# Where the split weights live in SBUF: `wh` and `wl` moved from the middle to the top

## Chip, cores and metric

One Trainium2 chip, one core. Times are device microseconds of that core; the time of a kernel is the median of its runs. The engines are TensorE (PE, with its weight loads shown apart as PEld), VectorE (DVE), ScalarE (ACT), GpSimd (POOL) and SyncE (SP), which here only issues DMAs.

## What is computed

Four transformer layers on 512 tokens of width 1024, in fp32: two layers of `first_block`, then two of `second_block`. Each has a mixer and a gated feed-forward unit, with a normalised residual after either. Cut to the matrix products:

```
first layer:   h = rms_norm(x)*(1+sc)+sh;  parts = split(h @ w_in);  latent queries, sparse attention and mLSTM
               x += g * rms_norm(concat(att, hm) @ w_out)
               h = rms_norm(x)*(1+sc)+sh;  x += g * rms_norm((silu(h @ w_gate) * (h @ w_up)) @ w_down)
second layer:  h = rms_norm(x);  parts = split(h @ w_in);  compressed, selected and window attention, stick-breaking attention
               y = g_a*(o_nsa @ w_proj_nsa) + g_b*(o_sb @ w_proj_sb);  x += rms_norm(y @ w_out)
               h = rms_norm(x);  u = conv(h @ w_up);  x += rms_norm((gelu(gate) * up) @ w_down)
```

The hidden width of the feed-forward units is 2816.

## The kernel before

Activations lie feature-major: a tile such as `hh` is [128, 8, 512], 8 chunks of 128 features by 512 tokens, 2048 bytes a chunk in each partition. Every large product is computed in three passes. Weights and activations are each split in a rounded head and the rest: `wh` and `wl` for the weights, `hh` and `hl` (mixers, gate/up), `cqh` and `cql` (latent queries), `fnh`/`fnl` and `fsh`/`fsl` (features of the second mixer, in its projections) or `hidh` and `hidl` (down projection) for the activations. `three_pass` (L198 to L201) issues three fp32r matmuls into one PSUM bank: head by head (L199), the weights' head by the activations' rest (L200), the weights' rest by the activations' head (L201). Each matmul has its own weight load: 128 columns of `wh` or `wl` are loaded and stay, and the activations' 512 columns stream. In the profile's names the streaming tile stands first and the loaded one second, as in `bank<-hh,wh`.

The weights come as a stream of slots of 128 x 1024 (L136 to L195). SP fills the ring `raw` of four slots by DMA (L160). ACT writes the head of a half slot (512 columns) to `wh` (L171), POOL subtracts it from `raw` and writes `wl` (L182); both have room for two slots. TensorE waits for the half slot's `wl`, uses it in 12 matmuls, and releases it through `slot_done`; ACT then refills it for the slot after next. Semaphores for all of this are written out by hand, and the order of each engine is the order of the code.

Most products load weights and stream activations. In three places `wh` and `wl` stream instead, and activations are loaded: the token-major values of the first mixer (L831 to L833, 512 columns) and of the second (L1775 to L1777, 512 or 280 columns), and the compression product of the second mixer, where 128 columns of `wh` or `wl` stream against 32 columns of `peh` or `pel` (through `three_pass`, so also L199 to L201).

`Arena` (L91) hands out addresses in a partition one after the other, rounded up to 32 bytes. `fixed` begins at base0 and holds, in this order, `x`, `hh`, `hl`, `y`, `raw`, `wh`, `wl`, the constants `cst`, parameters, `cos`, `sin`, `sq`, `acc` and `tmp`. The top MIX = 90112 bytes, from mix0 on, are a region that the mixers and the gated units use in turn: `hidh` and `hidl` fill it in the gate/up and down stages; in the mixers it holds the attention's tiles (`qk`, `pr`, `vsw`, `peh`), and then `fnh` to `fsl`. Further arenas overlay `y`, `sq` and `tmp`. `product_out` (L289) is the product with 1024 output features that ends each mixer (streaming `hh`, `hl`) and each gated unit (streaming `hidh`, `hidl`); `gate_up` (L505) is the first half of a gated unit. L1692 transposes through an identity in `cst` that streams, with `pr` or `sq` loaded.

Of the kernel before, what the change touches and what calls it, by code (L numbers as in the profile page):

```python
# [7 lines left out]
F32R = mybir.dt.float32r  # L8
# [5 lines left out]
P = 128  # L14
# [8 lines left out]
SLOT = 1024  # L23
# [180 lines left out]
def build(nc, a, out):  # L204

    m = Mem()
    base0 = -(-nc.sbuf_base // 32) * 32
    total = nc.sbuf_usable_end // 32 * 32 - base0
    MIX = KF * T * 4 * 2
    fixed = Arena(nc, base0, total - MIX)  # L210
    mix0 = base0 + total - MIX
    m.x = fixed("x", [P, KD, T])
    m.hh = fixed("hh", [P, KD, T], F32R)
    m.hl = fixed("hl", [P, KD, T], F32R)
# [1 line left out]
    m.y = fixed("y", [P, KD, T])  # L216
    ring_at = fixed.at
    m.raw = fixed("raw", [P, RING, SLOT])
    m.wh = fixed("wh", [P, 2, SLOT], F32R)
    m.wl = fixed("wl", [P, 2, SLOT], F32R)  # L220
    RING_BYTES = fixed.at - ring_at
    m.cst = fixed("cst", [P, C_COLS])
    m.pc = fixed("pc", [P, B_COLS])
# [2163 lines left out]
def program(nc, a, out):  # L2387
    build(nc, a, out)
# [150 lines left out]
```

How the kernel before makes its waits and increments, by code:

```python
    def __call__(self, ins):  # L111
        self.n += 1
        ins.then_inc(self.sem, 1)
        self.eng.wait_ge(self.sem, self.n)
# [40 lines left out]
    def loads(self, sp, t0, t1):  # L155
        for t in range(t0, min(t1, self.total)):
            if t >= RING:
                sp.wait_ge(self.rest_ready, 2 * (t - RING) + 2)
            w_ = self.width(t)
            sp.dma_start(self.m.raw[:, t % RING, 0:w_], self.source(t)[:, 0:w_]).then_inc(self.w_in[t % RING], 16)
# [4 lines left out]
    def head(self, act, t, half):  # L165
        if half == 0:
            act.wait_ge(self.w_in[t % RING], 16 * (t // RING + 1))
        if t >= 2:
            act.wait_ge(self.slot_done[half], t - 1)
        w_ = self.part(t, half)
        act.activation(self.m.wh[:, t % 2, w_], self.m.raw[:, t % RING, w_], ACT.Copy)\
           .then_inc(self.head_ready, 1)
# [6 lines left out]
    def rest(self, pool, t, half):  # L179
        pool.wait_ge(self.head_ready, 2 * t + half + 1)
        w_ = self.part(t, half)
        pool.tensor_tensor(self.m.wl[:, t % 2, w_], self.m.raw[:, t % RING, w_],
                           self.m.wh[:, t % 2, w_].bitcast(F32), ALU.subtract)\
            .then_inc(self.rest_ready, 1)
# [6 lines left out]
    def ready(self, pe, t, half=1):  # L191
        pe.wait_ge(self.rest_ready, 2 * t + half + 1)
# [1 line left out]
    def done(self, eng, t):  # L194
        eng.wait_ge(self.slot_done[1], t + 1)
# [109 lines left out]
        def tensor(pe):  # L305
# [15 lines left out]
                if part == 0 and nb >= 2:  # L321
                    pe.wait_ge(square_ready, nb - 1)
                    pe.wait_ge(y_ready, nb - 1)
                c0 = 8 * part
```

## Time and profile before

| | |
|---|---|
| median of 3 runs | 3337.89 us (3336.79 to 3338.76) |
| the profiled execution | 3341.34 us, its span 3339.6 us |
| TensorE's mean granted clock in it | 0.959 |
| busy: PE, PEld | 3135.7 us (94%), 2473.8 us (74%) |
| busy: DVE, ACT, POOL | 1577.1 us (47%), 1274.4 us (38%), 1300.4 us (39%) |

Busy time of a matmul counts from its start to its end, and matmuls are pipelined, so that one that "takes" 389 ns is followed by the next long before it ends. How far apart they start is read from the start times. A row of the groups ends with the idle time of the engine before its instructions and what ended it.

### The profile page before, as it was taken

To read this page: it belongs to the slowest core of one execution; us is meant where nothing else is said; L and a number is where in the kernel's file an instruction comes from. 1 tells how busy PE (TensorE), PEld (TensorE's weight loads), DVE (VectorE), ACT (ScalarE), POOL (GpSimd) and SP (SyncE) were. 2 spreads that over 40 slices of the span, in tenths; PEclk is the share of its full clock that TensorE was granted. 3 is DMA by queue.
4 is the path that set the end of the run, shared out by engine and by line. 5 is a ranking of instruction groups with operands and counts; after the bars stand their busy time and mean duration, and the time that the engine had idled before them with its cause. 6 is when DMAs were issued, how large, how long until landed. Compare 5 with 4: busy or idle time off the path is not lost.

```text
span 3339.6 us, 39384 instructions
## 1 busy us (share of the span) xinstructions
PE 3135.7 (94%) x14764; PEld 2473.8 (74%) x14764; DVE 1577.1 (47%) x2533; ACT 1274.4 (38%) x2494; POOL 1300.4 (39%) x1118
## 2 busy tenths in 40 slices
PE   5998789998989989998999998999989999989998
PEld 3666668886767768886877786888868777768886
DVE  7687466612776354212344644554043345355521
ACT  3335332233345432233353533443234534344432
POOL 2331235543432234443541542544434334434443
PEclk8998789998999889999999998999989999989998
DMA  5422336732411122322321121333223211223222
GB/s 209 120 77 89 120 131 237 250 99 72 123 64 45 39 73 96 100 92 73 119 87 45 45 76 57 101 95 100 93 82 101 74 45 51 90 67 96 95 93 71
DMA packets 92829, 316.50 MB, mean 95 GB/s; under 512 B 12000, under 2 KB 12512, under 8 KB 92512
## 3 DMA queue, kind: packets, MB, share of 16 engines
q1 hardware_dynamic: 92640, 313.99, 29.0%
q8 instruction: 118, 1.93, 0.2%
q14 instruction: 71, 0.58, 0.1%
HBM read 301.36 MB, written 2.10 MB: 91 GB/s over the span
## 4 chain that ended last, share of the span: by engine, by line
PE 90%; DVE 5%; issue 2%; ACT 1%; DMA 1%; SPq 1%; POOL 0%; DVEq 0%; ACTq 0%; POOLq 0%
PE bank L199 24%; PE bank L201 23%; PE bank L200 23%; PE bank L1713 3%; PE bank L1671 2%; PE bank L1692 2%; PE bank L412 1%; PE bank L813 1%; PE bank L831 1%; PE bank L833 1%; PE bank L832 1%; PE bank L975 1%; DMA mod_raw<-in_wmod 1%; DVE x L479 1%; DVE tmp L477 1%
## 5 line engine op out<-in xcount | busy, mean ns | idle before, releaser
L182 POOL TENSOR_TENSOR wl<-raw,wh 128x512 fp32r<-128x512 f32 (+1 forms) x952 | 1240.8, 1307 | 1917.8 <-ACT wh L171 1915.4
L171 ACT ACTIVATE wh<-raw 128x512 fp32r<-128x512 f32 (+1 forms) x952 | 587.4, 623 | 1471.8 <-PE bank L201 1363.8
L199 PE MATMUL bank<-hh,wh 128*128 128x512 f32 x2496 | 1005.2, 403 | 71.1 <-DVE hl L456 46.0
L201 PE MATMUL bank<-hh,wl 128*128 128x512 f32 x2496 | 984.3, 394 | 0.0
L200 PE MATMUL bank<-hl,wh 128*128 128x512 f32 x2496 | 983.4, 394 | 0.0
L199 PEld LDWEIGHTS bank<-hh,wh 128*128 128x128 f32 x2496 | 476.5, 191 | 196.8 <-DVE hl L456 51.8
L201 PEld LDWEIGHTS bank<-hh,wl 128*128 128x128 f32 x2496 | 475.1, 190 | 102.4
L200 PEld LDWEIGHTS bank<-hl,wh 128*128 128x128 f32 x2496 | 476.7, 191 | 96.2 <-issue 0.5
L201 PE MATMUL bank<-hidh,wl 128*128 128x512 f32 x704 | 281.1, 399 | 0.0
L200 PE MATMUL bank<-hidl,wh 128*128 128x512 f32 x704 | 277.6, 394 | 0.0
L199 PE MATMUL bank<-hidh,wh 128*128 128x512 f32 x704 | 276.1, 392 | 0.0
L371 DVE TENSOR_TENSOR acc<-acc,sq 128x512 f32<-128x512 f32 x48 | 41.2, 858 | 454.7 <-ACT sq L360 454.7
L200 PEld LDWEIGHTS bank<-hidl,wh 128*128 128x128 f32 x704 | 132.2, 188 | 34.4
L199 PEld LDWEIGHTS bank<-hidh,wh 128*128 128x128 f32 x704 | 132.2, 188 | 31.5
L201 PEld LDWEIGHTS bank<-hidh,wl 128*128 128x128 f32 x704 | 132.2, 188 | 30.4
L595 DVE SCALAR_TENSOR_TENSOR up<-bank,pc,up 128x511 f32<-128x511 f32 x88 | 65.9, 749 | 160.2 <-ACT up L575 158.4
L637 DVE CAST hidh<-hidden 128x512 fp32r<-128x512 f32 x88 | 122.7, 1394 | 3.0
L412 PE MATMUL bank<-sq,cst 128*128 128x512 f32 x128 | 78.5, 768 | 43.0 <-ACT sq L426 42.9
L635 DVE TENSOR_TENSOR hidden<-gate,bank 128x512 f32<-128x512 f32 x44 | 30.1, 683 | 169.1 <-PE bank L201 157.8
L1839 ACT ACTIVATE tmp<-bank 128x128 f32<-128x128 f32 (+3 forms) x128 | 55.1, 437 | 138.5 <-PE bank L1713 137.1
L412 PEld LDWEIGHTS bank<-sq,cst 128*128 128x128 f32 x128 | 27.2, 240 | 98.5 <-ACT sq L426 68.5
L595 DVE SCALAR_TENSOR_TENSOR gate<-bank,pc,gate 128x511 f32<-128x511 f32 x88 | 65.9, 749 | 53.1 <-ACT gate L575 51.5
(360 smaller groups left out, 3891.8 us busy)
## 6 DMA issues: line engine op xcount, KB each, us to landing
raw<-in_w SPq DMA_DIRECT2D x444, 512.0 KB, 3.4
mod_raw2a<-in_wmod SPq DMA_DIRECT2D x28, 512.0 KB, 4.5
mod_raw2b<-in_wmod SPq DMA_DIRECT2D x28, 512.0 KB, 4.6
mod_raw<-in_wmod SPq DMA_DIRECT2D x24, 512.0 KB, 4.0
raw<-in_w SPq DMA_DIRECT2D x32, 384.0 KB, 3.0
first_mods<-in_wmod SPq DMA_DIRECT2D x16, 512.0 KB, 13.9
tmp<-rawb SPq DMA_DIRECT2D x72, 64.0 KB, 2.2
turn<-sine SPq DMA_DIRECT2D x56, 64.0 KB, 2.0
```

The source lines that it names most:

```text
L171: act.activation(self.m.wh[:, t % 2, w_], self.m.raw[:, t % RING, w_], ACT.Copy)\
L182: pool.tensor_tensor(self.m.wl[:, t % 2, w_], self.m.raw[:, t % RING, w_], self.m.wh[:, t % 2, w_].bitcast(F32), ALU.subtract)\
L199: pe.matmul(out, wh, xh, start=start, stop=False)
L200: pe.matmul(out, wh, xl, start=False, stop=False)
L201: return pe.matmul(out, wl, xh, start=False, stop=stop)
L412: pe.matmul(ps[4][:], ones, m.sq[:, k % 2, :], start=(k == 0), stop=(k == KD - 1))\
L595: return dve.scalar_tensor_tensor(buf[:, pair, shift:T], bank[:, 0:T - shift], m.pc[:, col:col + 1], buf[:, pair, shift:T], ALU.mult, ALU.add)
L637: step(dve.tensor_copy(hidh[:, q, :], hs[:, pair, :]))
L1671: pe.matmul(ps[one][:, 0:w_], q_, k_, start=True, stop=True).then_inc(score, 1)
L1692: ins = pe.transpose(ps[2 + one][:, kb * P:(kb + 1) * P], prs[i % 6][:, kb * P:(kb + 1) * P], ident)
L1713: ins = pe.matmul(bank[:, h * HD:(h + 1) * HD], m.tmp[:, one, kb * P:(kb + 1) * P], v_, start=(kb == 0), stop=(kb == tb))
L1839: act.activation(m.tmp[:, one, 0:w_], ps[2 + one][:, 0:w_], ACT.Copy)\
```

## The change

`wh` and `wl` (8192 bytes each in a partition: two slots of 1024 elements) no longer come from `fixed` but from an arena of their own, `parts`, of 16384 bytes at the very top, above the shared region. The shared region moves down by those 16384 bytes, and so does all that lay behind `wl` in `fixed`; `x` to `raw` stay. The code that uses the tiles is the same:

```diff
-    fixed = Arena(nc, base0, total - MIX)
-    mix0 = base0 + total - MIX
+    PARTS = 2 * 2 * SLOT * 4
+    fixed = Arena(nc, base0, total - MIX - PARTS)
+    mix0 = base0 + total - MIX - PARTS
+    parts = Arena(nc, mix0 + MIX, PARTS)
...
     m.raw = fixed("raw", [P, RING, SLOT])
-    m.wh = fixed("wh", [P, 2, SLOT], F32R)
-    m.wl = fixed("wl", [P, 2, SLOT], F32R)
+    m.wh = parts("wh", [P, 2, SLOT], F32R)
+    m.wl = parts("wl", [P, 2, SLOT], F32R)
     RING_BYTES = fixed.at - ring_at
```

RING_BYTES is not used elsewhere.

## Rows read from the trace of the kernel before

**Rows 1.** The page's busy times (part 1) and chain of waits (part 4).
```profile
PE 3135.7 (94%) x14764; PEld 2473.8 (74%) x14764; DVE 1577.1 (47%) x2533; ACT 1274.4 (38%) x2494; POOL 1300.4 (39%) x1118
...
PE 90%; DVE 5%; issue 2%; ACT 1%; DMA 1%; SPq 1%; POOL 0%; DVEq 0%; ACTq 0%; POOLq 0%
PE bank L199 24%; PE bank L201 23%; PE bank L200 23%; PE bank L1713 3%; PE bank L1671 2%; PE bank L1692 2%; PE bank L412 1%; PE bank L813 1%; PE bank L831 1%; PE bank L833 1%; PE bank L832 1%; PE bank L975 1%; DMA mod_raw<-in_wmod 1%; DVE x L479 1%; DVE tmp L477 1%
```

**Rows 2.** Groups by line: line, engine, tiles, count | busy us, mean ns | idle before.
```profile
L199 PE MATMUL bank<-hh,wh 128*128 128x512 f32 x2496 | 1005.2, 403 | 71.1 <-DVE hl L456 46.0 <-issue 13.9 <-ACT vm L1064 6.2
L201 PE MATMUL bank<-hh,wl 128*128 128x512 f32 x2496 | 984.3, 394 | 0.0
L200 PE MATMUL bank<-hl,wh 128*128 128x512 f32 x2496 | 983.4, 394 | 0.0
...
L199 PE MATMUL bank<-hidh,wh 128*128 128x512 f32 x704 | 276.1, 392 | 0.0
```

**Rows 3.** Timeline of PE, L199: start us, duration us; ten starts each, first and last.
```profile
1249.91 0.39 PE L199 MATMUL bank<-hh,wh 128*128 128x512 f32 x1
...
1256.03 0.39 PE L199 MATMUL bank<-hh,wh 128*128 128x512 f32 x1
...
1460.07 0.39 PE L199 MATMUL bank<-hidh,wh 128*128 128x512 f32 x1
...
1466.36 0.39 PE L199 MATMUL bank<-hidh,wh 128*128 128x512 f32 x1
```

**Rows 4.** Windows in gate/up, down, output product: busy (count) by engine, PEclk, DMA.
```profile
1300.00:1420.00 120.00, 120.00 (x531) 99.40 (x530) 34.18 (x36) 33.49 (x57) 56.80 (x44) 1.00 0.30 97
1436.00:1556.00 120.00, 120.00 (x516) 96.54 (x515) 8.36 (x11) 37.78 (x65) 55.62 (x47) 1.00 0.29 94
2015.00:2045.00 30.00, 30.00 (x134) 24.87 (x133) 4.13 (x5) 13.17 (x23) 14.34 (x12) 1.00 0.28 88
```

**Rows 5.** Groups of L199: whole span (`fnh`), 1300 to 1420 us (`hh`), 1436 to 1556 us.
```profile
L199 PE MATMUL bank<-fnh,wh 128*128 128x512 f32 x64 | 25.1, 393 | 0.0
...
L199 PE MATMUL bank<-hh,wh 128*128 128x512 f32 x177 | 68.9, 389 | 0.0
...
L199 PE MATMUL bank<-hidh,wh 128*128 128x512 f32 x172 | 67.4, 392 | 0.0
```

**Rows 6.** The group of L199 with `cqh` streaming.
```profile
L199 PE MATMUL bank<-cqh,wh 128*128 128x512 f32 x32 | 13.2, 413 | 3.6 <-issue 3.6
```

**Rows 7.** Timeline of PE in the compression product, L199: seven starts, first and last.
```profile
1700.92 0.23 PE L199 MATMUL bank<-wh,peh 128*32 128x128 f32 x1
...
1702.00 0.22 PE L199 MATMUL bank<-wh,peh 128*32 128x128 f32 x1
```

**Rows 8.** L1692, transposes: its two groups, and four in a row in the timeline.
```profile
L1692 PE MATMUL bank<-cst,pr 128*128 128x128 f32 x320 | 49.2, 284 | 1.4 <-DVEq L2029 1.3
L1692 PE MATMUL bank<-cst,sq 128*128 128x128 f32 x160 | 24.4, 283 | 1.4 <-DVEq L2029 1.4
...
1728.75 0.60 PE L1692 MATMUL bank<-cst,pr 128*128 128x128 f32 x4
```

**Rows 9.** Groups in which `wh` streams, shapes kept apart.
```profile
L831 PE MATMUL bank<-wh,hh 128*128 128x512 f32 x128 | 53.4, 417 | 12.7 <-issue 12.7
L1775 PE MATMUL bank<-wh,hh 128*128 128x512 f32 x64 | 24.9, 389 | 0.0
L199 PE MATMUL bank<-wh,peh 128*32 128x128 f32 x128 | 24.2, 226 | 0.0
```

**Rows 10.** ACT on two places, as groups; a head and a rest in the timeline.
```profile
L580 ACT ACTIVATE gate<-gate 128x512 f32<-128x512 f32 x44 | 27.3, 622 | 0.0
L1012 ACT ACTIVATE qk<-qk 128x512 f32<-128x512 f32 x16 | 10.0, 623 | 0.0
...
1250.79 0.63 ACT L171 ACTIVATE wh<-raw 128x512 fp32r<-128x512 f32 x1 [2.03 <-PE bank L201]
1251.50 1.29 POOL L182 TENSOR_TENSOR wl<-raw,wh 128x512 fp32r<-128x512 f32 x1 [1.37 <-ACT wh L171]
```

## The prediction

> **What bounds the kernel.** I read the shares of busy time and the chain of waits first [rows 1]. TensorE's matmuls are busy 94% of the span and are 90% of the chain; 70% of the chain lies on the three lines of the three-pass product (L199, L200, L201), and POOL, which makes `wl`, is 0% of it. The groups by line say the same of the waits [rows 2]: ahead of L200 and L201 TensorE's matmuls idled 0.0 us, ahead of L199 71.1 us of 3339.6, mostly for `hl` (VectorE). So the kernel is a long row of fp32r matmuls back to back, and its time is their number times their spacing. Whatever changes the spacing changes the time one for one; whatever changes ACT or POOL a little does not.
>
> The spacing must be read from starts, since the durations shown (389 to 399 ns) overlap. Starts of L199 with `hh` streaming lie 0.68 us apart, nine times running from 1249.91 to 1256.03 [rows 3]: 680 ns for the three matmuls, 226.7 ns each. With `hidh`/`hidl` streaming (down projection) nine steps take 6.29 us, 1460.07 to 1466.36: 699 ns, which I round to 700, 233 ns each [rows 3]. Same shape, same code, same weights' buffers, full clock in both. The stages agree [rows 4]: 531 matmuls in 120 us (226 ns) in a gate/up stage, 516 (233 ns) in a down stage. It is not the banks or the stage's code: the output product of a mixer runs the same function into the same banks 6 and 7 with `hh` streaming, and does 134 matmuls in 30 us (224 ns, by whole counts). And it is not the data: `fnh`, the mixer's features (`fsh` is its like), has the long duration too: 393 ns for L199, against 392 for `hidh` and 389 for `hh` at full clock [rows 5].
>
> What `hid*`, `fn*` and `fs*` (both halves of each) share is where they lie. From the code: base0 is 16512, the usable end 229344 in this build, so `x`, `hh`, `hl`, `y`, `raw`, `wh`, `wl` and all large tiles below the shared region start at multiples of 64 bytes (`wh` at 98432), and mix0 is 229344 - 90112 = 139232, which is 32 more than a multiple of 64. Every tile there starts 32 bytes off. The trace cannot say whether the 20 ns per three passes come from this offset or from lying high in memory, but one of them costs it.
>
> **The change, part by part.** No instruction, semaphore, wait or DMA is added, removed or reordered; RING_BYTES is used nowhere. Only addresses change. (1) From `cst` to `tmp`, and the shared region, everything moves down by 16384 bytes: offsets within any power of two up to that stay, so `hid*` stay 32 off. (2) `wh` goes to 212960 and `wl` to 221152, both 32 off and high. So the weights, so far aligned and low, get what the region's tiles have. The weights' tiles are the stationary operand of nearly all matmuls and the streaming one of a few.
>
> Stationary, with aligned `hh`, `hl` or `cq*` streaming: 2496 + 32 = 2528 triples [rows 2, 6]. The trace has no full-size row of "aligned streams, misplaced is loaded". The nearest is the compression product: `wh` streams 128 columns against 32 columns of `peh`, a tile of the shared region, 32 off. Its triples lie 180 ns apart, six from 1700.92 to 1702.00 [rows 7]: 60.0 ns each. What is beyond the streaming: 128 columns at 2.4 GHz are 53.3 ns; four transposes of 128 columns at two cycles a column take 0.60 us less the last one's 0.27 over three steps, 109 ns against 106.7 [rows 8], so 2.6 ns are a matmul's own. That leaves 4.1 ns for 32 loaded columns, 16.4 for 128. For `hh` with aligned weights it is 226.7 - 213.3 - 2.6 = 10.8 ns for 128. So misplaced weights cost some 5.6 ns a matmul more, 16 a triple (rounded down, because the small shape may hold a fixed part). Bounds: above 20 ns a triple, the one full-size price of misplacement [rows 3]; below, zero if the load does not care, and under zero, if a shift of the load against the stream avoids what makes 10.8 ns, at most -32 a triple. I take 16, the nearest row by kind: 2528 x 16 ns = 40.4 us. From it goes 1 us for stretches at half clock, since the stages that hold most of these matmuls run at 1.00 [rows 4] and their means exceed 389 little [rows 2].
>
> Streaming: `wh`/`wl` stream in 128 triples of L831 to L833 and 64 of L1775 to L1777 with 512 columns [rows 9]; I charge what `hid*` pays, 192 x 20 ns = 3.8 us. The 64 triples of L1775 to L1777 with 280 columns (a token tile's short half, by the code) and the 128 with `peh` [rows 9] get 0.5 us together (bounds 0 to 2). Sum 4.3 us, bounds 0 to 6.
>
> Both misplaced: `hid*` and `fn*`/`fs*` streaming, 704 + 128 = 832 triples (`fnh` 64 in [rows 5], `fsh` as many; `hidh` in [rows 2]). The penalty could vanish (the two now lie alike, as `hh` and `wh` do), stay, or double: -20, 0, +20 ns, so -16.6, 0, +16.6 us. I take 0, the middle.
>
> ACT's head and POOL's rest write and read the moved tiles. ACT needs 622 ns in place on aligned `gate` and 623 on `qk` in the misplaced region [rows 10], so no cost there. POOL has no such pair (bounds: none, or twice its 1.3 us), but a half buffer is freed three halves (8.2 us) before it is needed, and head plus rest take 0.63 + 1.3 us [rows 10]: at 2.6 us it still fits under its period of 2.7 us. DMA writes `raw` and the moved tiles at the same offsets as before: nothing.
>
> Sum: 40.4 - 1 + 4.3 + 0 = +44 us. The profiled execution took 3341.34 us (span 3339.6), 3.4 above the median 3337.89. On its basis 3385, on the median's 3382.
>
> A rule of the Trainium skill speaks against all of this. "SBUF — State Buffer", section "Who interferes with whom", says that only the shared port pair causes contention and that PE and ACT never wait on anyone; "TensorE: Matmul & The Clock Gate", Part 2, says that loading the next weights does not take read bandwidth from the running matmul. By them addresses matter to nothing here, and the time stays 3338; by the traced rows 20 ns a triple already hang on one placement, so the rules are at least incomplete; they are rival (d) below.
>
> **Rivals.** (a) Only the streaming operand's place counts; the weights' load does not care. For it: misplaced `pr` and aligned `sq` as stationary take 284 and 283 ns [rows 8]. Against it: those are the half-rate fp32 streams, which leave room, and the 180 ns of `peh` speak of the full-rate ones. Time: 3338 + 4 = 3342.
>
> (b) What counts is how the two lie against each other. Then `hh` pairs become unlike (+16 a triple) and `hid*` pairs alike (-20): 39.4 + 4.3 - 16.6 = +27, to +37 with 20 instead of 16: 3365 to 3375. For it: `hh` against `wh` is the fast pair and both are at multiples of 64. Against it: nothing in the trace separates it.
>
> (c) The other side, faster: the slow pairs of before are slow because a stream in the region meets loads from the low part, and an aligned stream is content with any load. Then `hid*` and `fn*`/`fs*` fall to 680 and `hh` stays: -16.6 + 4.3 = -12, 3326. It decides from the point where `hh` triples stay at 680 or below; if they also lose part of the 10.8 ns, every 5 ns a triple is another 12.6 us. For it: `cq*` at 65664, well away from `wh`, runs no slower than `hh`, so distance alone does no harm (its mean is 413 only by half-clock stretches [rows 6]). Against it: `peh`.
>
> (d) The moved weights cost nothing in either role: the 20 ns belong to those tiles for a reason that the rows hide, and the sum is 0: 3338. Against it: the same function and shape, differing in the streaming tile alone [rows 3, 4]. This is what the Trainium skill's two rules above would give.
>
> **How the numbers follow.** Forecast (aligned streams pay for misplaced weights, `hid*` about unchanged) 37%, its own range 3370 to 3410; (a) 27%; (b) 16%; (c) 16%; (d) 4%. The predicted time is the forecast's, 3382. No change from a change can be told here within 0.2%, 6.7 us. Slower: 37 + 16 + 3 of (a), whose 4 us may be 7: 0.56. Same: 24 of (a) and 4 of (d): 0.28. Faster: (c), 0.16. The range 3323 to 3400 takes in (a), (b), the main form of (c) and the forecast but for its uppermost part (`hid*` doubled), and leaves out (c)'s deeper form.
>
> **What would show it.** Right: starts of L199 with `hh` 0.69 to 0.70 us apart, and about 515 to 520 matmuls in 120 us of a gate/up stage; `hid*` still at 0.70; 512-column triples with `wh` streaming near 0.70; ACT, POOL, VectorE durations and all waits as before. (a) shows as 0.68 and 0.70, with only L831 to L833 and L1775 to L1777 longer; (b) as 0.70 and 0.68; (c) as 0.68 and 0.68. I am wrong in kind if spacings stand and the time differs, which would put the cause in a wait, for instance PE waiting for POOL's `wl`.

## The result, and the profile after

The changed kernel takes 3374.7 us (median of 4 runs, 3370.72 to 3380.01) against 3338.32 for the kernel before: ratio 1.0109, 95% interval 1.0091 to 1.0126, so some 36 us slower. Its profiled execution has a span of 3372.9 us and a mean granted clock of 0.961 (0.959 before).

The chain of waits has the same shape as in [rows 1], and the groups show no new wait: the rows that answer to [rows 2], and the head and rest (L171, L182).

```profile
L182 POOL TENSOR_TENSOR wl<-raw,wh 128x512 fp32r<-128x512 f32 (+1 forms) x952 | 1238.8, 1305 | 1953.5 <-ACT wh L171 1952.4
L199 PE MATMUL bank<-hh,wh 128*128 128x512 f32 x2496 | 1021.3, 409 | 72.5 <-DVE hl L458 46.0 <-issue 14.6 <-ACT vm L1066 6.2
L201 PE MATMUL bank<-hh,wl 128*128 128x512 f32 x2496 | 1001.1, 401 | 0.0
L200 PE MATMUL bank<-hl,wh 128*128 128x512 f32 x2496 | 1000.8, 401 | 0.0
L171 ACT ACTIVATE wh<-raw 128x512 fp32r<-128x512 f32 (+1 forms) x952 | 588.0, 623 | 1509.5 <-PE bank L201 1400.0 <-PE bank L835 56.1 <-PE bank L1779 49.3
...
L201 PE MATMUL bank<-hidh,wl 128*128 128x512 f32 x704 | 273.9, 389 | 0.0
L199 PE MATMUL bank<-hidh,wh 128*128 128x512 f32 x704 | 273.9, 389 | 0.0
L200 PE MATMUL bank<-hidl,wh 128*128 128x512 f32 x704 | 273.9, 389 | 0.0
```

The two rows of the kernel before that [rows 2] leaves out, for the down projection:

```profile
L201 PE MATMUL bank<-hidh,wl 128*128 128x512 f32 x704 | 281.1, 399 | 0.0
L200 PE MATMUL bank<-hidl,wh 128*128 128x512 f32 x704 | 277.6, 394 | 0.0
```

TensorE idled 72.5 us ahead of L199 (71.1 before) and 0.0 ahead of the others; POOL's mean is 1305 ns (1307 over all forms before). What moved are the matmuls themselves, and in both directions. With `hh`/`hl` streaming the three means rise by 6, 7 and 7 ns (403, 394, 394 in [rows 2]). With `hidh`/`hidl` they fall, from 392, 394 and 399 to 389 each. The starts say it in full (timeline of PE, L199: start, duration), for `hh` in a gate/up stage and `hidh` in a down stage, to be held against [rows 3]:

```profile
1330.11 0.40 PE L199 MATMUL bank<-hh,wh 128*128 128x512 f32 x1
...
1336.43 0.40 PE L199 MATMUL bank<-hh,wh 128*128 128x512 f32 x1
...
2349.97 0.39 PE L199 MATMUL bank<-hidh,wh 128*128 128x512 f32 x1
...
2356.09 0.39 PE L199 MATMUL bank<-hidh,wh 128*128 128x512 f32 x1
```

Nine triples of `hh` take 6.32 us, 702 ns each (680 before); nine of `hidh` take 6.12 us, 680 each (700 before). The fast and the slow pair have changed places. Where `wh` streams, these rows answer to [rows 9] (the change adds two lines, so L831 is now L833 and L1775 is L1777):

```profile
L833 PE MATMUL bank<-wh,hh 128*128 128x512 f32 x128 | 53.5, 418 | 11.1 <-issue 11.1
...
L1777 PE MATMUL bank<-wh,hh 128*128 128x512 f32 x64 | 25.3, 396 | 0.0
...
L199 PE MATMUL bank<-wh,peh 128*32 128x128 f32 x128 | 24.2, 226 | 0.0
```

They are slower where all 512 columns stream (396 against 389 in the second mixer), and the compression product has not moved (226 and 226).

The account: 2528 triples with `hh` or `cq*` at +20 ns, by the means of the groups (6 + 7 + 7), are +50.6 us; 832 triples with `hid*`, `fn*`, `fs*` at -20, by the starts (-18 by the means of the groups), are -16.6; `wh` and `wl` streaming 512 columns are +3 (the three lines of the first mixer, 128 each, rose from 417, 404, 404 to 418, 409, 412; those of the second, 64 each, from some 389 to some 395). Sum +37 us (39 with the -18), measured +36.4. Next to nothing is left over for a wait or another engine. The means of `hh` hold stretches at half clock too, which is why they give 20 where the starts at full clock give 22.

At half clock the place of `wh` costs `hh` nothing. In both kernels the stretch shown runs at a granted clock of 0.50, 1.2 GHz; the starts below are two triples apart, 1.28 us a triple or 427 ns a matmul, in the kernel before (first two lines) and after (last two), with `hh` and `wh` alike in the one and unlike in the other.

```profile
440.52 0.63 PE L199 MATMUL bank<-hh,wh 128*128 128x512 f32 x1
...
443.08 0.63 PE L199 MATMUL bank<-hh,wh 128*128 128x512 f32 x1
```
```profile
442.90 0.63 PE L199 MATMUL bank<-hh,wh 128*128 128x512 f32 x1
...
445.46 0.63 PE L199 MATMUL bank<-hh,wh 128*128 128x512 f32 x1
```

### The profile page after: what moved, and what is told of

It reads as the page before. It is cut to its first block, busy times and chain, and to the rows that moved or that the text cites. A ratio compares the mean times of both kernels' runs of the same rounds, so it can differ in the third digit from the quotient of the medians.

```text
span 3372.9 us, 39384 instructions
## 1 busy us (share of the span) xinstructions
PE 3169.3 (94%) x14764; PEld 2476.9 (73%) x14764; DVE 1584.6 (47%) x2533; ACT 1274.8 (38%) x2494; POOL 1298.3 (38%) x1118
## 4 chain that ended last, share of the span: by engine, by line
PE 89%; DVE 5%; issue 2%; DMA 1%; ACT 1%; SPq 1%; POOL 0%; DVEq 0%; ACTq 0%; POOLq 0%
PE bank L199 24%; PE bank L201 23%; PE bank L200 23%; PE bank L1715 3%; PE bank L414 2%; PE bank L1673 2%; PE bank L1694 2%; DMA mod_raw<-in_wmod 1%; PE bank L815 1%; PE bank L977 1%; PE bank L833 1%; PE bank L835 1%; PE bank L834 1%; DVE acc L446 1%; PE bank L1779 1%
## 5 line engine op out<-in xcount | busy, mean ns | idle before, releaser
L182 POOL TENSOR_TENSOR wl<-raw,wh 128x512 fp32r<-128x512 f32 (+1 forms) x952 | 1238.8, 1305 | 1953.5 <-ACT wh L171 1952.4
L171 ACT ACTIVATE wh<-raw 128x512 fp32r<-128x512 f32 (+1 forms) x952 | 588.0, 623 | 1509.5 <-PE bank L201 1400.0
L199 PE MATMUL bank<-hh,wh 128*128 128x512 f32 x2496 | 1021.3, 409 | 72.5 <-DVE hl L458 46.0
L201 PE MATMUL bank<-hh,wl 128*128 128x512 f32 x2496 | 1001.1, 401 | 0.0
L200 PE MATMUL bank<-hl,wh 128*128 128x512 f32 x2496 | 1000.8, 401 | 0.0
L199 PEld LDWEIGHTS bank<-hh,wh 128*128 128x128 f32 x2496 | 478.1, 192 | 213.0 <-DVE hl L458 51.8
L201 PEld LDWEIGHTS bank<-hh,wl 128*128 128x128 f32 x2496 | 477.8, 191 | 116.9
L200 PEld LDWEIGHTS bank<-hl,wh 128*128 128x128 f32 x2496 | 478.9, 192 | 110.8 <-issue 0.5
L201 PE MATMUL bank<-hidh,wl 128*128 128x512 f32 x704 | 273.9, 389 | 0.0
L199 PE MATMUL bank<-hidh,wh 128*128 128x512 f32 x704 | 273.9, 389 | 0.0
L200 PE MATMUL bank<-hidl,wh 128*128 128x512 f32 x704 | 273.9, 389 | 0.0
L199 PEld LDWEIGHTS bank<-hidh,wh 128*128 128x128 f32 x704 | 132.2, 188 | 27.7
L201 PEld LDWEIGHTS bank<-hidh,wl 128*128 128x128 f32 x704 | 132.2, 188 | 27.3
L200 PEld LDWEIGHTS bank<-hidl,wh 128*128 128x128 f32 x704 | 132.2, 188 | 27.3
```

The costliest lines, as they stand in the source:

```text
L171: act.activation(self.m.wh[:, t % 2, w_], self.m.raw[:, t % RING, w_], ACT.Copy)\
L182: pool.tensor_tensor(self.m.wl[:, t % 2, w_], self.m.raw[:, t % RING, w_], self.m.wh[:, t % 2, w_].bitcast(F32), ALU.subtract)\
L199: pe.matmul(out, wh, xh, start=start, stop=False)
L200: pe.matmul(out, wh, xl, start=False, stop=False)
L201: return pe.matmul(out, wl, xh, start=False, stop=stop)
```

## The experiments

Each kernel was timed beside the kernel before on the same chip. Two windows serve for all of them: 1330 to 1420 us lies in a gate/up stage (`hh` streams) and 2345 to 2415 us in a down stage (`hidh`, `hidl` stream). Their columns are as in [rows 4], and what is read is the first count, PE's matmuls. The two lines of the kernel before and of the changed one:

```profile
1330.00:1420.00 90.00, 90.00 (x399) 74.55 (x398) 23.08 (x24) 25.05 (x43) 42.60 (x33) 1.00 0.31 100
2345.00:2415.00 70.00, 70.00 (x301) 56.33 (x300) 4.11 (x5) 21.94 (x38) 32.83 (x29) 1.00 0.31 96
```
```profile
1330.00:1420.00 90.00, 90.00 (x386) 72.36 (x385) 23.08 (x25) 24.12 (x40) 41.26 (x33) 1.00 0.29 94
2345.00:2415.00 70.00, 70.00 (x310) 58.01 (x309) 6.97 (x9) 22.45 (x39) 32.74 (x29) 1.00 0.33 108
```

Before: 399 and 301, fast and slow. After: 386 and 310, slow and fast. 399 in 90 us and 310 in 70 are 226 ns; 386 and 301 are 233. (A window also counts the matmuls that its ends cut; by the starts it is 227, and 234 and 233.) In r3, r4 and r6 to r9 the tiles behind the weights move up by 32 or 64 bytes too; all matmuls in the two windows are those of `three_pass`.

**The region alone moved to a multiple of 128 (r1).**

```diff
-    mix0 = base0 + total - MIX
+    mix0 = (base0 + total - MIX) // 128 * 128
```

> The kernel before, with the shared region alone moved down by 96 bytes, to 139136, a multiple of 128; wh and wl stay in the middle at 98432. Theory O (offset): a fp32r matmul is slow when the streaming tile and the loaded tile start at different offsets within 64 bytes. Then hid* and fn*/fs* against wh/wl fall from 700 to 680 ns a triple, hh stays at 680, and the time is 3338 - 832 x 20 ns = 3322 us. Rival R (region): it is slow when one of the two lies in the upper part of SBUF and the other in the lower. Then hid* stays at 700 and the time at 3338 us.

Measured: 3317.26 us against 3337.38, ratio 0.9941 (0.9926 to 0.9956), so 20 us faster. The windows:

```profile
1330.00:1420.00 90.00, 90.00 (x399) 74.53 (x398) 24.90 (x26) 24.76 (x41) 42.94 (x34) 1.00 0.28 93
2345.00:2415.00 70.00, 70.00 (x311) 57.96 (x310) 4.34 (x5) 21.96 (x38) 33.91 (x29) 1.00 0.29 98
```

Both stages are fast, with the region still high and the weights still low. 96 bytes, and no engine's work changed. The theory of the offset stands, that of the region falls: it wanted 301 in the second line.

**The changed kernel with region and top moved down by 96 bytes (r2).** As r1, applied to the changed kernel:

```diff
-    mix0 = base0 + total - MIX - PARTS
+    mix0 = (base0 + total - MIX - PARTS) // 128 * 128
```

> The changed kernel, with the shared region and the weights above it moved down by 96 bytes (region at 122752, wh at 212864, both multiples of 128): the weights are as high as in the changed kernel but aligned like hh. Theory O: all pairs at 680 ns a triple, 3322 us, some 53 us below the changed kernel. Rival R: hh low against wh high stays at 703, hid* high against wh high at 680, 3375 us.

Measured: 3316.37 us, ratio 0.9937 (0.9923 to 0.9952); 399 and 311 matmuls in the windows. The weights are at the top and nothing is slow. So the move to the top is not what cost 36 us, but the place at which it ended: 32 bytes past a multiple of 64.

**`wh` and `wl` moved by 32 bytes, left in the middle (r3).**

```diff
+    fixed.at += 32
     m.wh = fixed("wh", [P, 2, SLOT], F32R)
     m.wl = fixed("wl", [P, 2, SLOT], F32R)
+    fixed.at += 32
```

> The kernel before, with wh and wl moved up by only 32 bytes (to 98464 and 106656), still in the middle; the region stays at 139232. Theory O: hh against wh becomes unlike, hid* against wh alike: hh at 700 to 703 ns, hid* at 680, 3370 to 3376 us, the whole effect of the change without its move. If what counts is the difference within 128 bytes (stream minus load), hh minus wh is -32, that is 96, the same as hid* minus wh in the kernel before, and hh triples take 700 ns without spread, where the changed kernel has 32 and 703. Rival R: 680 for hh, 700 for hid*, 3338 us.

Measured: 3376.26 us, ratio 1.0120 (1.0105 to 1.0135), the time of the change without its move. But half of the expectation fails:

```profile
1330.00:1420.00 90.00, 90.00 (x387) 72.48 (x386) 23.29 (x25) 24.41 (x41) 41.26 (x32) 1.00 0.28 94
2345.00:2415.00 70.00, 70.00 (x302) 56.70 (x301) 7.28 (x9) 22.64 (x39) 31.99 (x28) 1.00 0.31 106
```

`hh` is slow as expected, and `hid*` stays slow (302), though `hidh` and `wh` are now both 32 off within 64 bytes. Within 128 they are 96 and 32. So a period of 64 bytes is too short. Nor is `hid*` equally slow everywhere: in the first down stage of this kernel, with the same addresses, the window of 70 us has 308 matmuls (229 ns by the starts), where the third has 302.

```profile
710.00:780.00 70.00, 70.00 (x308) 57.42 (x307) 3.38 (x5) 20.92 (x36) 32.21 (x28) 1.00 0.28 96
```

**By 64 bytes (r4).**

```diff
+    fixed.at += 64
     m.wh = fixed("wh", [P, 2, SLOT], F32R)
```

> The kernel before, with wh and wl moved up by 64 bytes (98496 and 106688); the region stays at 139232. Theory O with a period of 64 bytes: hh at 680 as before, hid* at 700, 3338 us. With a period of 128 bytes: hh against wh becomes unlike (700 or another figure, +50 us for 20 ns a triple) and hid* minus wh becomes 32 (703): about 3390 us. Rival R: 3338 us, as before.

Measured: 3378.09 us, ratio 1.0121 (1.0102 to 1.0139), with 388 and 302 matmuls. `hh` and `wh` are both multiples of 64 here and the pair is slow: a period of 64 is out. The 3390 expected of the longer period charged 20 ns to each of the 2528 triples; by the means of the groups it is 16 here (408, 400 and 399 ns against 403, 394 and 394), and the products with `wh` streaming slowed little (L1778, `hl` loaded, has a mean of 388 ns in this kernel, as if alike).

**By 128 bytes, modulo 256 (r5).** On r1, `cst` and `pc` are allocated ahead of `wh`, which shifts `wh` and `wl` by 8320 bytes, and the tiles behind them stay:

```diff
+    m.cst = fixed("cst", [P, C_COLS])
+    m.pc = fixed("pc", [P, B_COLS])
     m.wh = fixed("wh", [P, 2, SLOT], F32R)
     m.wl = fixed("wl", [P, 2, SLOT], F32R)
...
-    m.cst = fixed("cst", [P, C_COLS])
-    m.pc = fixed("pc", [P, B_COLS])
```

> The kernel with the region at a multiple of 128 (r1), and with cst and pc (8320 bytes, 65 x 128) placed ahead of wh instead of behind wl. Every large tile stays at a multiple of 128, but wh and wl now differ from hh, hl and hid* by an odd number of 128 bytes, where they differed by an even number. If the period of the offset is 128 bytes: all triples at 680 ns, 3317 us as r1. If it is 256 bytes or more: all pairs unlike, 2528 + 832 + 192 triples at about 700, 3317 + 71 = 3388 us.

Measured: 3374.46 us against 3338.84, ratio 1.0117 (1.0098 to 1.0136).

```profile
1330.00:1420.00 90.00, 90.00 (x389) 72.98 (x388) 23.08 (x24) 24.45 (x41) 42.12 (x33) 1.00 0.29 94
2345.00:2415.00 70.00, 70.00 (x303) 56.76 (x302) 2.96 (x4) 21.55 (x37) 33.05 (x28) 1.00 0.34 112
```

All large tiles are multiples of 128 and both stages are slow (231 ns by the counts, 232 by the starts). A period of 128 is out too. The price is 57 us over r1, less than the 71 expected: 16 ns for each of the 3552 triples, those at half clock included, not 20.

**By 256 bytes' multiples, as a control (r10).** As r5, with `mod` moved ahead as well, a shift of 8704 bytes:

```diff
     m.cst = fixed("cst", [P, C_COLS])
     m.pc = fixed("pc", [P, B_COLS])
+    m.mod = fixed("mod", [P, 48 * LAYERS])
     m.wh = fixed("wh", [P, 2, SLOT], F32R)
```

> A control for the kernel with wh and wl 128 bytes off by modulo 256 (r5): the same move of cst and pc ahead of wh, and mod with them, so that the shift is 8704 bytes, 34 x 256. If the slot in a period of 256 bytes is all that counts, every 512-column triple is back at 680 ns and the time at 3317 us, as with the region alone moved (r1). If the reordering itself cost the time of r5, this kernel is slow too, 3374 us.

Measured: 3316.21 us against 3337.93, ratio 0.9927 (0.9909 to 0.9946).

```profile
1330.00:1420.00 90.00, 90.00 (x398) 74.53 (x398) 23.86 (x26) 24.81 (x42) 42.82 (x34) 1.00 0.30 97
2345.00:2415.00 70.00, 70.00 (x310) 57.98 (x309) 4.34 (x5) 22.09 (x39) 34.59 (x29) 1.00 0.30 98
```

The same reordering, 384 bytes further, and all is fast. It is the place within 256 bytes that counts, and r5's cost is not one of the order. (r2 had shown that a further difference of 256 modulo 512 does no harm: `hh` starts at 128 modulo 512 there and `wh` at 384.)

**By 16 and by 4 bytes (r6, r8).** Both weights' parts in one tile, whose contents begin 4 or 1 elements late. `Shifted` (its class is left out here) adds this number to every column index; the cut shows r6, and r8 has 1 in place of 4:

```diff
-    m.wh = fixed("wh", [P, 2, SLOT], F32R)
-    m.wl = fixed("wl", [P, 2, SLOT], F32R)
+    both = fixed("wh", [P, 4 * SLOT + 8], F32R)
+    m.wh, m.wl = Shifted(both, 4), Shifted(both, 4 + 2 * SLOT)
```

> The kernel before with wh and wl in one tile, their contents 16 bytes behind a multiple of 128 (both parts then bear the name wh in the trace). If what counts is which piece of 32 bytes or more an access falls in, 16 bytes less or more split pieces but keep the order, and hh stays near 680: 3338 us. If any difference counts down to 16 bytes: hh near 700, 3338 + 51 + 4 = 3393 us at most, hid* (80 away) at 700 as before.

> As r6, with the contents of wh and wl 4 bytes behind a multiple of 128. If a difference counts only from 32 bytes on: 3338 us, hh at 680. If every difference counts: hh near 700, up to 3393 us. If accesses are by lines of 16 bytes, the shift splits lines and may cost more than 16 bytes do.

Measured: 16 bytes, 3362.62 us, ratio 1.0069 (1.0050 to 1.0089); 4 bytes, 3397.37 us, ratio 1.0175 (1.0160 to 1.0190), the slowest of all. At 4 bytes `hid*` is slower than in any other kernel, 298 matmuls in its window, and `hh` has 389:

```profile
2345.00:2415.00 70.00, 70.00 (x298) 55.91 (x297) 11.61 (x15) 23.23 (x39) 26.74 (x27) 1.00 0.28 94
```

At 16 bytes the same pair is fast in one gate/up stage and slow in another (windows in the second layer's and in the third's):

```profile
1330.00:1420.00 90.00, 90.00 (x398) 74.51 (x397) 23.71 (x25) 25.01 (x42) 42.57 (x33) 1.00 0.30 99
2150.00:2240.00 90.00, 90.00 (x387) 72.87 (x387) 47.60 (x57) 35.10 (x56) 41.28 (x32) 1.00 0.29 94
```

398 against 387, with the same addresses. So the offset alone does not fix the cost, as r3 showed for `hid*`: one pair of addresses can run at more than one spacing, and what picks it is not shown. With 4 bytes the compression product is a little longer too: the mean of L199 (there L210) with `peh` is 228 ns, where it is 225 to 227 in every other kernel.

**`wl` alone, and `wh` alone, 32 bytes off (r7, r9).** In the first, `wh` is like `hh` and `wl` is not; in the second, with the order swapped, `wl` is.

```diff
     m.wh = fixed("wh", [P, 2, SLOT], F32R)
+    fixed.at += 32
     m.wl = fixed("wl", [P, 2, SLOT], F32R)
+    fixed.at += 32
```

```diff
-    m.wh = fixed("wh", [P, 2, SLOT], F32R)
     m.wl = fixed("wl", [P, 2, SLOT], F32R)
+    fixed.at += 32
+    m.wh = fixed("wh", [P, 2, SLOT], F32R)
+    fixed.at += 32
```

> The kernel before with wl alone moved up by 32 bytes; wh stays like hh. Each triple runs: wh loaded, hh streams (L199); wh loaded, hl streams (L200); wl loaded, hh streams (L201). Theory C (collision): what costs is the load that is read while a tile streams, that is the NEXT matmul's weights; then the spacing after L200 grows (wl is loaded beneath it) from 227 to 232 or more, and those after L199 and L201 stay at 227. Rival W (own weights): the spacing after L201, whose own weights are wl, grows and that after L200 stays. Either way about a third of the effect for hh: 2528 x 7 ns = 18 us, minus what hid* against wl gives back (832 x 7 ns = 6 us): 3350 us.

> The kernel before with wl and wh in swapped order: wl at 98432, like hh; wh 32 bytes off, at 106656. After the kernel with wl alone off (any mismatch among the three cost hh the full 20 ns a triple, 12 of them after L200, beneath which wl is loaded), theory C (collision of a stream with the load read beneath it) expects the excess for hh after L199 and L201, beneath which wh is loaded, and little after L200; the triple again near 700 ns. Rival W (a matmul is slow by its own loaded tile) expects the excess after L199 and L200. Time: hh 2528 x 20 = +51 us, the rest about level, about 3375 to 3390 us in either.

Measured: 3375.03 us, ratio 1.0106 (1.0091 to 1.0121), for `wl`; 3369.47 us, ratio 1.0093 (1.0078 to 1.0108), for `wh`, a little under the 3375 expected at least. One unlike part costs nearly as much as two (r3, 1.0120), which I had not expected of r7 (3350). Where the time goes is seen in the groups of 1330 to 1420 us, mean ns of one last but one; 389 is the value of alike pairs [rows 5]. `wl` off, then `wh` off:

```profile
L200 PE MATMUL bank<-hl,wh 128*128 128x512 f32 x129 | 51.6, 400 | 0.0
L199 PE MATMUL bank<-hh,wh 128*128 128x512 f32 x129 | 51.0, 395 | 0.0
L201 PE MATMUL bank<-hh,wl 128*128 128x512 f32 x129 | 50.2, 389 | 0.0
```
```profile
L201 PE MATMUL bank<-hh,wl 128*128 128x512 f32 x130 | 51.3, 395 | 0.0
L199 PE MATMUL bank<-hh,wh 128*128 128x512 f32 x130 | 51.2, 394 | 0.0
L200 PE MATMUL bank<-hl,wh 128*128 128x512 f32 x130 | 51.0, 393 | 0.0
```

With `wl` off, L201, the only one whose own weights are off, is untouched (389), and L200, beneath which `wl` is loaded, has the most (+11). The ends of matmuls are modelled, but the starts in this window agree: the next matmul follows L199 after 232 ns, L200 after 239 and L201 after 229, where it is 226 to 227 for all three in the kernel before. So a matmul is not slow by its own weights, and rival W falls. Theory C, a collision of the stream with the load read beneath it, gets two thirds of it right, but not the +6 of L199, nor in the second kernel the +4 of L200, whose load is of the like `wl`. The second kernel, with +4 to +6 everywhere, tells C from W no further. And an excess can be uneven with no difference between the three pairs: `hid*` in the kernel before has 392, 394 and 399 ns with all three 96 bytes apart. So C is not shown. Either a delay shifts what comes after against its own load, or C is not all of it.

## Why the prediction was right in sum and wrong in its mechanism

The time, 3374.7, lies in the range and on the side forecast (3382). The spacings do not: `hh` at 0.70 and `hid*` at 0.68 is the sign that the prediction had set for its rival (b). By its own steps:

- That TensorE is the bound, that nothing but spacing could move, and that ACT, POOL, DMA and the waits would not: right. L171 stayed at 623 ns, and the idle time ahead of L199 grew by 1.4 us.
- `hh` with misplaced weights, +16 ns a triple, +39 us: the sign right, the size short. It was +20 by the groups' means, +50.6 us, and 22 in the stretch read by starts, which is over the upper bound of 20. It rested on `peh`, and that row was no witness: its mean is 226 ns in the kernel before, in the changed one and in r5, with `wh` at 128, 224 and 0 modulo 256 and `peh` at 96, 96 and 0 (and its slices, 128 bytes apart, alternate between two places anyway). The excess of 4.1 ns for 32 columns cannot be put down to misplacement.
- Both misplaced, `hid*` unchanged, 0: wrong, and this is the step that fails. It was -20 ns a triple, -16.6 us, the lower bound. I called 0 "the middle" and had no row for it.
- `wh` streaming, +4.3 us: about +3.
- The two errors, +11 and -17 us, nearly cancel; that 3382 is near is luck.

What holds is rival (b): the two tiles' places against each other. Its upper end, with 20 instead of 16, was 3375. I had written that nothing in the trace separates it. That is so, but it needed one price for both traced facts (a pair with no difference is fast, a pair with one is slow), while the forecast had to add a second price for misplaced weights. Rival (a), the stream alone, fell by `hid*`, whose offset did not change and which became fast. Rival (c) fell by `hh`.

Rival (d) was what the Trainium skill gives ("SBUF — State Buffer", "Who interferes with whom": PE and ACT never wait on anyone). Its 3338 fell by 36 us. No other engine is needed for what is seen here, so that sentence may stand for waits between engines. That loading the next weights takes no read bandwidth from the running matmul (the Trainium skill, "TensorE: Matmul & The Clock Gate", Part 2) is hard to square with r7: of the products' tiles only `wl` was moved, and L199 and L200, which do not use it, went from 389 ns to 395 and 400. The runs show time, not bandwidth, so by what means the load acts stays open.

What stays open: by what in the memory the difference acts, why alike tiles still need 227 ns where 512 columns at 2.4 GHz are 213, and what picks the spacing at 16 bytes and in r3. The loads' own durations do not tell (187 to 188 ns in the gate/up window before, after and in r7), and no run here took the weight loads away.

## What to carry to other kernels

In a row of fp32r matmuls back to back at full clock, with 512 columns streaming, let the streaming tile and the loaded tile start at the same place within 256 bytes; here one line that rounds a region's start down (r1, 96 bytes) gave 0.6%, and an unlucky address cost 1.1%. When one group of matmuls has a longer spacing than another of the same shape, list the addresses of both operands before looking for a wait. And an address change is judged by pairs of operands, not by one of them.

## What the runs showed that I had not expected

The spacing of the matmuls by the difference of start addresses, stream less load, modulo 256, for `hh` or `hid*` against `wh` in steps of 32 (mean distance of the starts at full clock, in kernels where both weights' parts are shifted alike):

| difference | pair, kernel | ns a matmul |
|---|---|---|
| 0 | `hh` before, r1, r2, r10; `hid*` after, r1, r2, r10 | 227 |
| 32 | `hid*` r4 | 233 |
| 64 | `hid*` r3 | 229 in the first and last down stage, 233 in the others |
| 96 | `hid*` before | 233 |
| 128 | both r5 | 232 |
| 160 | `hh` after | 234 |
| 192 | `hh` r4 | 233 |
| 224 | `hh` r3 | 233 |

The cost is not graded by distance: one place in eight is fast, the others cost 6 to 8 ns a matmul, but for the two stages at 64 with 2. Finer steps are no help (16 bytes: fast or slow by stage; 4 bytes: the slowest kernel). At half clock, 427 ns, the difference is gone for `hh`. And with one of the two weights' parts unlike, the triple is as slow or nearly as slow as with both.
